# Layer 0's causal attention with the mLSTM head norms, the last modulation folds and half of tile 0's output projection placed inside it

## The chip, the cores and the metric

The kernel runs on one core of a Trainium2 chip. The metric is the device time of one execution in microseconds (us), lower is better. The engines are PE (TensorE, matrix products), DVE (VectorE), ACT (ScalarE), POOL (GpSimd) and SP (which only issues DMA transfers); each works through its own program in order, and they wait for each other by semaphores. Everything is float32.

## What is computed

Two blocks, 256 tokens of width 1024. Block 1 has two layers; the change lies in the mixer of layer 0, an mLSTM (4 heads of 128) beside a causal attention (8 heads of 64):

```python
h = rms_norm(x, norm_mix_g) * (1 + sc1) + sh1      # sh1, sc1, g1, sh2, sc2, g2 from silu(c) @ ada_w + ada_b
z = h @ w_in                                       # mq, mk, mv, mo, gates, bq, bk, bv
hm = mlstm_chunkwise(mq, mk, mv, i_pre, f_pre)
hm = rms_norm(hm, mnorm_g) * sigmoid(mo)           # per mLSTM head
qb, kb = rms_norm(bq, qn_g), rms_norm(bk, kn_g)    # per attention head
hb = softmax(qb @ kb.T / 8 - slope * distance, causal) @ bv     # 8 heads
x = x + g1 * (concat(hm, hb) @ w_out)
h = rms_norm(x, norm_ffn_g) * (1 + sc2) + sh2
x = x + g2 * peer_ffn(h)                           # 128 expert rows of u and v gathered per token
```

With 256 tokens and blocks of 256 keys, the reference's `moba_attention` has no past block to choose, so it is this plain causal attention. After it come layer 1 (differential attention, PEER again) and block 2 (three attentions and a mixture of experts).

## The kernel before

Tokens lie in two tiles of 128 (`T` = 2). `hT` holds the transposed input of the projections, 8 chunks of 128 features by 256 tokens; for the output projection `out0` chunks 0 to 3 are the mLSTM's heads and 4 to 7 the attention's, two heads in each. Every engine's program is written out by hand, so the order of the lines is the order of the work. What stands around the change, by line of the profile:

- **Projections.** `project` on PE (L946 to L988) and `move` on ACT (L1814) work through weight slots of 2 MB that SP loads into a ring of four (L741), each when its old user is done. `out0` is two slots of 512 columns, and per slot and tile 8 products 128x512 (L969). Two PSUM banks `gp` take turns.
- **Modulation of later layers.** Some vectors of `ada_w` are summed on DVE (`weigh`, L2516 to L2520, one per slot) and some on PE: the `mix` slots, 8 steps numbered 0 to 7, "part" (8 products, L946) or "fold" (2 products, L952 and L953). Steps 6 and 7 are folds.
- **mLSTM** (`mlstm`, PE L1248, ACT L1968, DVE L2572). For each of 4 heads: scores (L1258 to L1261), log weights on DVE (L2582), exp on ACT (L1976), weights (L2593), weights times values (L1280), and `divide` on DVE (L2601 to L2606), which writes the head into `y`. `mix` steps stand between the heads.
- **Norms of the attention's q and k.** Four blocks of 4 heads each (q 0 to 3, q 4 to 7, k 0 to 3, k 4 to 7). PE spreads the inverse roots over the rows (`head_spread`, L1060, through the two banks `tp`), DVE multiplies (`head_scale`, L2383).
- **Attention** (`attention("moba")`, PE L1170, ACT L1904, DVE L2465). One unit per head; per unit and tile: score products (L1182, four banks: two of `sp_`, two of `gp`), bias and row maximum on DVE (L2482, L2492), exp with row sum on ACT (L1928), reciprocal on DVE (L2499), division on POOL (`divide_rows`, L850), three transposes on PE (L1195, banks `tp`), copy by ACT (L1918, L1919), two value products per unit (L1209), and a copy of every pair of heads into `hT` by DVE (L2504). The loop keeps the transposes three units behind the scores. It begins when all q and k blocks are scaled and all `mix` steps moved.
- **mLSTM head norms.** Squares and sums on DVE ahead of the attention (L2627, L2628), the root on ACT (L1984), then `mlstm_scale` on DVE near the attention's end: per tile three passes of 128x512 (L2640 to L2642: times the inverse root, times `mnorm`, times the sigmoid `mo_sig`). PE turns the result into `hT` (L1014).
- **Behind it.** `out0` for tile 0 and tile 1, two `weigh` steps on DVE meanwhile, `first_residual` (L2648), `first_norm` (to L2662), the transposes of `h`, the queries of the PEER layer (`wq0`, L974), the top 16 of the scores (`topk`, L2668 to L2717), and the gather of expert rows by POOL (L909), 512 gathers of 1 MB over both layers.

## Time and profile before

| | before |
|---|---|
| median of 3 runs | 2408.13 us (2406.37 to 2408.23) |
| the profiled execution, its time | 2415.83 us |
| its span in the trace | 2414.0 us |
| PE busy | 2037.4 us, 84% |
| DVE busy | 1296.4 us, 54% |
| ACT busy | 835.6 us, 35% |
| POOL busy | 650.2 us, 27% |
| chain that ended last | PE 48%, DMA 35%, DVE 8%, ACT 6% |
| DMA | 932.78 MB, mean 386 GB/s |

The profile's page gives such totals over the whole span. The chain is followed back from the last instruction, each step to what released it. Since the stages have different limits, the timeline and the windows of the stage around the change (185 to 290 us) are what the next sections read. In a timeline row, "x8" counts records: a float32 product leaves two.

### The profile page before, as it was taken

To read this page: it belongs to the slowest core of one execution; us is meant where nothing else is said; L and a number is where in the kernel's file an instruction comes from. 1 tells how busy PE (TensorE), PEld (TensorE's weight loads), DVE (VectorE), ACT (ScalarE), POOL (GpSimd) and SP (SyncE) were. 2 spreads that over 40 slices of the span, in tenths; PEclk is the share of its full clock that TensorE was granted. 3 is DMA by queue.
4 is the path that set the end of the run, shared out by engine and by line. 5 is a ranking of instruction groups with operands and counts; after the bars stand their busy time and mean duration, and the time that the engine had idled before them with its cause. 6 is when DMAs were issued, how large, how long until landed. Compare 5 with 4: busy or idle time off the path is not lost.

```text
span 2414.0 us, 26478 instructions
## 1 busy us (share of the span) xinstructions
PE 2037.4 (84%) x9050; PEld 1072.1 (44%) x9050; DVE 1296.4 (54%) x3180; ACT 835.6 (35%) x2261; POOL 650.2 (27%) x601
## 2 busy tenths in 40 slices
PE   6997988798799899789989878988889996667676
PEld 3553732354265357256455423544447543222222
DVE  4866686767756775864867768455433421111111
ACT  1223254444534644443644435333323410000000
POOL 1001145433423433532433444434430300000000
PEclk9998999999999999999999999999999988888878
DMA  9984699999999999999999999999997269999998
GB/s 378 365 346 168 268 420 421 421 421 420 411 393 421 418 395 420 421 409 421 408 389 411 421 421 421 421 421 421 421 373 268 101 275 428 428 428 428 428 429 377
DMA packets 110268, 932.78 MB, mean 386 GB/s; under 512 B 12710, under 2 KB 14020, under 8 KB 16644
## 3 DMA queue, kind: packets, MB, share of 16 engines
q0 software_dynamic: 76800, 549.70, 55.6%
q1 hardware_dynamic: 33348, 381.60, 38.3%
q8 instruction: 61, 1.00, 0.2%
q14 instruction: 59, 0.48, 0.1%
HBM read 930.15 MB, written 6.06 MB: 388 GB/s over the span
## 4 chain that ended last, share of the span: by engine, by line
PE 48%; DMA 35%; DVE 8%; ACT 6%; issue 2%; POOL 1%; SPq 0%; DVEq 0%; POOLq 0%
DMA arena<-in_peer_uv_dram,arena 19%; PE summed L1323 18%; DMA arena<-in_moe_pieces_dram 15%; PE gp L1395 6%; PE gp L969 4%; DVE y_g L2733 4%; PE gp L988 2%; PE gp L1391 2%; PE gp L1686 2%; PE gp L979 2%; ACT arena L2019 1%; PE gp L1524 1%; PE gp L946 1%; ACT arena L2016 1%; PE gp L1073 1%
## 5 line engine op out<-in xcount | busy, mean ns | idle before, releaser
L1323 PE MATMUL summed<-arena 128*128 128x512 f32 x2048 | 987.4, 620 | 187.2 <-ACT arena L2019 165.8
L2733 DVE CUSTOM_DVE_ANT_0 y_g<-arena,h 128x1024 f32<-128x1024 f32 x512 | 627.1, 1225 | 409.2 <-DMA arena<-in_peer_uv_dram,arena 352.1
L909 POOL DMA_INDIRECT arena<-in_peer_uv_dram,arena x512 | 590.8, 1154 | 946.6 <-PE summed L1323 856.1
L1323 PEld LDWEIGHTS summed<-arena 128*128 128x128 f32 x2048 | 373.1, 195 | 699.5 <-ACT arena L2019 340.3
L2013 ACT ACTIVATE arena<-arena 128x1 f32<-128x1 f32 x512 | 102.2, 200 | 510.7 <-DVE arena L2733 509.8
L1686 PE MATMUL gp<-arena,mod 128*32 128x512 f32 x1008 | 161.6, 776 | 107.7 <-DMA arena<-in_moe_pieces_dram 107.7
L2019 ACT ACTIVATE arena<-cst,arena 128x128 f32<-128x128 f32 x512 | 205.5, 401 | 16.8
L3113 DVE TENSOR_TENSOR mod<-mod,gp 128x512 f32<-128x512 f32 x8 | 5.5, 688 | 367.5 <-ACT mod L2282 367.5
L2016 ACT ACTIVATE arena<-arena 128x1 f32<-128x1 f32 x512 | 150.8, 295 | 17.7 <-DVE arena L2722 1.1
L1686 PEld LDWEIGHTS gp<-arena,mod 128*32 128x32 f32 x1008 | 31.8, 126 | 229.3 <-DMA arena<-in_moe_pieces_dram 172.2
L969 PE MATMUL gp<-arena,hT 128*128 128x512 f32 x224 | 100.0, 606 | 1.1 <-issue 0.6
L2282 ACT ACTIVATE mod<-gp 128x512 f32<-128x512 f32 x8 | 4.8, 597 | 261.1 <-PE gp L1686 261.1
L1395 PEld LDWEIGHTS gp<-hT,mod 128*128 128x128 f32 x640 | 74.5, 192 | 9.8 <-issue 8.4
L1395 PEld LDWEIGHTS gp<-hT,arena 128*128 128x128 f32 x640 | 74.6, 192 | 9.6 <-issue 9.6
L2520 DVE SCALAR_TENSOR_TENSOR h<-arena,cst,h 128x512 f32<-128x512 f32 x98 | 73.7, 752 | 3.5
L1395 PE MATMUL gp<-hT,mod 128*128 128x128 f32 x640 | 74.8, 275 | 0.0
L1395 PE MATMUL gp<-hT,arena 128*128 128x128 f32 x640 | 74.7, 275 | 0.0
L969 PEld LDWEIGHTS gp<-arena,hT 128*128 128x128 f32 x224 | 43.0, 194 | 56.2 <-issue 55.2
L1814 ACT ACTIVATE arena<-gp 128x512 f32<-128x512 f32 (+1 forms) x29 | 17.1, 590 | 144.5 <-PE gp L988 41.2
L1661 PE MATMUL summed<-mod,h 128*128 128x128 f32 x256 | 46.3, 364 | 22.5 <-DVE mod L3108 22.4
L2668 DVE MAX8 arena<-arena 128x8 f32<-128x128 f32 (+1 forms) x192 | 58.4, 332 | 11.7 <-ACT arena L1998 8.4
L2013 ACT ACT_TABLE_LOAD x50 | 64.2, 1283 | 0.9
(468 smaller groups left out, 2162.3 us busy)
## 6 DMA issues: line engine op xcount, KB each, us to landing
arena<-in_moe_pieces_dram SPq DMA_DIRECT2D x95, 2048.0 KB, 25.6
arena<-in_w_slots_dram SPq DMA_DIRECT2D x47, 2048.0 KB, 10.1
arena<-in_w_parts_dram SPq DMA_DIRECT2D x45, 1024.0 KB, 9.2
mod<-in_w_parts_dram SPq DMA_DIRECT2D x29, 1024.0 KB, 9.3
arena<-in_peer_uv_dram,arena POOLq DMA_INDIRECT x512, 14.2
t_rep<-t_rows POOLq DMA_DIRECT2D x1, 3066.0 KB, 12.9
arena<-t_rep POOLq DMA_DIRECT2D x1, 2304.0 KB, 11.1
y_g<-in_moe_pieces_dram SPq DMA_DIRECT2D x1, 2048.0 KB, 17.8
```

What stands on the lines that cost most here:

```text
L909: pool.indirect_dma_start(rowbuf[b], None, a["peer_uv"].rearrange("l n d -> (l n) d"), bass.IndirectOffsetOnAxis(ap=idx[:, col(n):col(n) + ...
L969: mm = pe.matmul(bank, hT[:, k, grp[1] * P:(grp[1] + 1) * P], w[:, k, :], start=k == 0, stop=k == KT - 1)
L979: mm = pe.matmul(bank[:, c * P:(c + 1) * P], w[:, k, grp[1] + c * P:grp[1] + (c + 1) * P], hT[:, k, P:S], start=k == 0, stop=k == KT - 1)
L1323: mm = pe.matmul(op[:, b, :], diag[:, n % DIAGS, :], rowbuf[n % ROWS][:, D + b * 512:D + (b + 1) * 512], start=n % SLOTS == 0, stop=n % SL ...
L1395: mm = pe.matmul(bank[:, c * P:(c + 1) * P], w[:, k, c * P:(c + 1) * P], hT[:, k, tok], start=k == 0, stop=k == KT - 1)
L1686: mm = pe.matmul(gp[c, j, :], xe[:, 2 * kk + k, c], w[:, e, k, :], start=kk + k == 0, stop=kk == 3 and k == 1, skip_group_check=True)
L2013: link(act.activation(gelu[:, c:c + 1], dots[:, c:c + 1], ACT.Gelu))
L2016: link(act.activation(coef[:, c:c + 1], gelu[:, c:c + 1], ACT.Copy, scale=gate[:, c:c + 1]))
L2019: act.activation(diag[:, n % DIAGS, :], ident, ACT.Copy, scale=coef[:, c:c + 1]).then_inc(diag_ready, 1)
L2520: ins = v.scalar_tensor_tensor(out=acc, in0=w[:, k, :], scalar=cact[:, k:k + 1], in1=acc, op0=ALU.mult, op1=ALU.add)
L2668: ins = v.max(b[:, part], s)
L2733: v.tensor_tensor_reduce(y[:, t, :], rowbuf[n % ROWS][:, 0:D], h[:, t, :], 1.0, 0.0, ALU.mult, ALU.add, dots[:, c:c + 1]).then_inc(udot, 1)
```

## The change

All of it is order and placement in layer 0; the result is the same sum.

- **PE.** `mix` steps 6 and 7 leave the mLSTM, and the spreads of q 0 to 3 and k 0 to 3 stand there instead. `attention` becomes `causal_attention`, written out for pairs of heads: scores in the two `sp_` banks only, which leaves the `gp` banks to folds 6 and 7 and to two groups of `out0`. The first half (chunks 0 to 3, the mLSTM's part) of tile 0's two `out0` groups stands inside the attention, ahead of and behind the transposes of pair 2; the second halves follow the attention.
- **DVE.** The first two head scales stand before `divide(3)`, the others after the bias of pair 0. Squares are gone; the sums (`memory_squares`) and the scaling (`memory_scale`) stand inside the attention. Scaling is one pass per head of 128x128, because the `mnorm` factor is already in `mo_sig`.
- **POOL.** `gate_and_square` ahead of the divisions: `mo_sig` times `mnorm` (128x1024) and the two squares (128x512 each).
- **ACT.** The sigmoid comes before folds 6 and 7, the root of the head norms after the exps of pair 0, so there are two loads of the exp table in the attention. The order of the blocks in `QK` lets pairs 0 and 1 start after two blocks.

```diff
+causal = att["moba"][1]
+causal_home = [work[:, CH * j:CH * (j + 1)] for j in range(4)] + [tk[:, CH * j:CH * (j + 1)] for j in range(3)] + [work[:, 0:CH]]
...
-QK = {"moba": [(8, G_EVQ), (10, G_EVQ), (12, G_EVK), (14, G_EVK)],
+QK = {"moba": [(8, G_EVQ), (12, G_EVK), (10, G_EVQ), (14, G_EVK)],
...
+    def gate_and_square():
+        pool.wait_ge(sig_done, 1)
+        pool.wait_ge(lam_in, 48)
+        pool.tensor_tensor(mo_sig, mo_sig, mnorm.unsqueeze(1).to_broadcast([P, T, CH]), ALU.mult).then_inc(sig_done, 1)
+        pool.wait_ge(mm_read, M_HEADS)
+        for t in range(T):
+            pool.tensor_tensor(h[:, t, 0:CH], y[:, t, 0:CH], y[:, t, 0:CH], ALU.mult).then_inc(hn_sq, 1)
+    def divide_causal():
+        for j in range(len(causal)):
+            pool.wait_ge(d_inv, j + 1)
+                rows = causal_logits(j, t)
+                k = 2 * (j % 4) + t
+                ins = pool.tensor_tensor(rows, rows, den[:, k:k + 1].to_broadcast([P, (t + 1) * P]), ALU.mult)
...
+    def causal_scores(p):
+        pe.wait_ge(qk_done, 2 if p < 2 else 4)
+        for j in (2 * p, 2 * p + 1):
+            sg = causal[j]
+            if j >= 2:
+                pe.wait_ge(s_read, j - 1)
...
+    def causal_turn(p):
+        for j in (2 * p, 2 * p + 1):
+            pe.wait_ge(scale_ready, j + 1)
+            if j >= 2:
+                pe.wait_ge(t_moved, j - 1)
+            else:
+                pe.wait_ge(qk_done, 4)
...
+    def causal_values(p):
+        for j in (2 * p, 2 * p + 1):
+            pe.wait_ge(t_moved, j + 1)
+            if p >= 2:
+                pe.wait_ge(o_read, p - 1)
...
+    def turn_memory_out(t):
+        pe.wait_ge(ml_normed, t + 1)
+        pe.wait_ge(t_moved, 3 + 3 * t)
+        turn_rows(y[:, t, :], 1)
+    def out0_tile0(m, k0, k1):
+        n = phase_slots["out0"][m]
+        g = group_of[n, 0]
+        w = ring[:, place[n], :].rearrange("p (k c) -> p k c", k=KT)
+        if k0 == 0:
+            pe.wait_ge(w_landed[place[n]], 16 * (use[n] + 1))
+            pe.wait_ge(gemm_moved, g - 1)
+        for k in range(k0, k1):
+            mm = pe.matmul(gp[:, g % 2, :], hT[:, k, 0:P], w[:, k, :], start=k == 0, stop=k == KT - 1)
+        if k1 == KT:
+            mm.then_inc(gemm_done, 1)
+    def causal_attention():
+        causal_scores(0)
+        mix(6)
+        head_spread("moba", 2)
+        head_spread("moba", 3)
+        causal_scores(1)
+        mix(7)
+        causal_turn(0)
+        causal_scores(2)
+        causal_values(0)
+        causal_turn(1)
+        turn_memory_out(0)
+        causal_scores(3)
+        causal_values(1)
+        hT_ready()
+        out0_tile0(0, 0, 4)
+        causal_turn(2)
+        out0_tile0(1, 0, 4)
+        causal_values(2)
+        turn_memory_out(1)
+        hT_ready()
+        causal_turn(3)
+        causal_values(3)
...
-            mix(2 * hh + 1)
+                mix(2 * hh + 1)
+            else:
+                pe.wait_ge(mm_arg, M_HEADS)
+                head_spread("moba", 0)
+                head_spread("moba", 1)
...
-            mix(2 * hh + 2)
+            if hh < 2:
+                mix(2 * hh + 2)
...
-    pe.wait_ge(mm_arg, M_HEADS)
-    for i in range(len(QK["moba"])):
-        head_spread("moba", i)
-    pe.wait_ge(qk_done, len(QK["moba"]))
-    pe.wait_ge(gemm_moved, group_end(mix_slots[-1]))
-    attention("moba")
+    causal_attention()
-    for t in range(T):
-        project("out0", tile=t)
+    out0_tile0(0, 4, 8)
+    out0_tile0(1, 4, 8)
+    project("out0", tile=1)
...
+    def causal_attention():
+        causal_exp(0, 1)
+        mix(6)
+        act.wait_ge(hn_sq, 3)
+        act.activation(small[:, 32:40], small[:, 24:32], ACT.Sqrt).then_inc(hn_rt, 1)
+        mix(7)
+        causal_moved(0)
+        causal_exp(2, 3)
+        causal_moved(1)
+        causal_exp(4, 5)
+        move_turned_rows(0, 1)
+        causal_moved(2)
+        causal_exp(6, 7)
+        move_turned_rows(1, 1)
+        causal_moved(3)
...
-        mix(6)
-        mix(7)
-        act.wait_ge(hn_sq, 1)
-        act.activation(small[:, 32:40], small[:, 24:32], ACT.Sqrt).then_inc(hn_rt, 1)
...
+    def causal_bias(p):
+        for j in (2 * p, 2 * p + 1):
+            bias = causal[j]["bias"]
+            k = 2 * (j % 4)
+            v.wait_ge(s_done, j + 1)
+            if j == 7:
+                v.wait_ge(t_done, 1)
+            for t in range(T):
+                ins = v.scalar_tensor_tensor(out=causal_logits(j, t), in0=bias[1][t], scalar=bias[2],
+                                             in1=sp_[:, j % 2, t * S:t * S + (t + 1) * P], op0=ALU.mult, op1=ALU.add)
+            ins.then_inc(s_read, 1)
+            v.wait_ge(s_read, j + 1)
+            if j >= 4:
+                v.wait_ge(scale_ready, j - 3)
+            for t in range(T):
+                ins = v.tensor_reduce(nmax[:, k + t:k + t + 1], causal_logits(j, t), AX.X, ALU.max, negate=True)
+            ins.then_inc(m_done, 1)
...
+    def causal_attention():
+        causal_bias(0)
+        head_scale("moba", 2)
+        head_scale("moba", 3)
+        causal_inverse(0, 1)
+        memory_squares()
+        causal_bias(1)
+        memory_scale(0)
+        causal_inverse(2, 3)
+        causal_bias(2)
+        causal_out(0)
+        memory_scale(1)
+        causal_inverse(4, 5)
+        causal_out(1)
+        causal_bias(3)
+        causal_inverse(6, 7)
+        causal_out(2)
+        causal_out(3)
+        v.wait_ge(o_read, 4)
...
+        head_scale("moba", 0)
+        head_scale("moba", 1)
-        head_scales("moba")
-        yh = y[:, :, 0:512].rearrange("p t (h n) -> p t h n", h=M_HEADS)
+    def memory_squares():
-            link(v.tensor_tensor(sq[:, t], yh[:, t], yh[:, t], ALU.mult))
-            link(v.tensor_reduce(small[:, 24 + t * M_HEADS:24 + (t + 1) * M_HEADS], sq[:, t], AX.X, ALU.add))
+            v.wait_ge(hn_sq, t + 1)
+            ins = v.tensor_reduce(small[:, 24 + t * M_HEADS:24 + (t + 1) * M_HEADS], sq[:, t], AX.X, ALU.add)
+        link(ins)
-    def mlstm_scale():
-        yh = y[:, :, 0:512].rearrange("p t (h n) -> p t h n", h=M_HEADS)
-        v.wait_ge(hn_rt, 1)
-        link(v.reciprocal(small[:, 32:40], small[:, 32:40]))
-        r = small[:, 32:40].rearrange("p (t h) -> p t h", t=T)
-        v.wait_ge(sig_done, 1)
-        v.wait_ge(lam_in, 48)
-        for t in range(T):
-            link(v.tensor_tensor(yh[:, t], yh[:, t], r[:, t, :].unsqueeze(2).to_broadcast([P, M_HEADS, M_DH]), ALU.mult))
-            link(v.tensor_tensor(y[:, t, 0:512], y[:, t, 0:512], mnorm, ALU.mult))
-            link(v.tensor_tensor(y[:, t, 0:512], y[:, t, 0:512], mo_sig[:, t, :], ALU.mult))
-        v.sem_inc(ml_normed, 1)
+    def memory_scale(t):
+        if t == 0:
+            v.wait_ge(hn_rt, 1)
+            link(v.reciprocal(small[:, 32:40], small[:, 32:40]))
+            v.wait_ge(sig_done, 2)
+        for hh in range(M_HEADS):
+            rows = y[:, t, P * hh:P * (hh + 1)]
+            k = 32 + M_HEADS * t + hh
+            ins = v.scalar_tensor_tensor(out=rows, in0=rows, scalar=small[:, k:k + 1], in1=mo_sig[:, t, P * hh:P * (hh + 1)],
+                                         op0=ALU.mult, op1=ALU.mult)
+        ins.then_inc(ml_normed, 1)
```

On PE, from the values of mLSTM head 2 to the first scores; `summed` are the values, `gp` the folds, `turned` the spreads, `scores` the attention. Before:

```order
L1280 MATMUL summed<-ones,arena 128x1 x3
L952 MATMUL gp<-h,cst 1x512
L953 MATMUL gp<-ada_b,cst 1x512
L952 MATMUL gp<-h,cst 1x512
L953 MATMUL gp<-ada_b,cst 1x512
L1280 MATMUL summed<-arena 128x128 x3
L1280 MATMUL summed<-ones,arena 128x1 x3
L1060 MATMUL turned<-arena,cst 64x512 x8
L1182 MATMUL scores<-arena 128x128
```

Now:

```order
L1302 MATMUL summed<-ones,arena 128x1 x3
L1049 MATMUL turned<-arena,cst 64x512 x4
L1302 MATMUL summed<-arena 128x128 x3
L1302 MATMUL summed<-ones,arena 128x1 x3
L1167 MATMUL scores<-arena 128x128
L1167 MATMUL scores<-arena 128x256
L1167 MATMUL scores<-arena 128x128
L1167 MATMUL scores<-arena 128x256
L941 MATMUL gp<-h,cst 1x512
L942 MATMUL gp<-ada_b,cst 1x512
L1049 MATMUL turned<-arena,cst 64x512 x4
```

The two folds left the mLSTM, two of the four spreads took their place, and the first pair's scores stand ahead of a fold and of the other spreads.

On PE, the attention's last part; `turned<-cst,arena` are the weights of a pair, `summed` its values, `gp<-arena,hT` the output projection, `turned<-cst,y_g` the mLSTM's heads. Before:

```order
L1195 MATMUL turned<-cst,arena 128x128 x3
L1209 MATMUL summed<-y_g,arena 64x256
L1209 MATMUL summed<-y_g,arena 64x128
L1209 MATMUL summed<-y_g,arena 64x256
L1209 MATMUL summed<-y_g,arena 64x128
L1014 MATMUL turned<-cst,y_g 128x128 x8
L1209 MATMUL summed<-y_g,arena 64x256
L1209 MATMUL summed<-y_g,arena 64x128
L969 MATMUL gp<-arena,hT 128x512 x32
```

Now:

```order
L1213 MATMUL gp<-arena,hT 128x512 x4
L1181 MATMUL turned<-cst,arena 128x128 x6
L1213 MATMUL gp<-arena,hT 128x512 x4
L1194 MATMUL summed<-y_g,arena 64x256
L1194 MATMUL summed<-y_g,arena 64x128
L1194 MATMUL summed<-y_g,arena 64x256
L1194 MATMUL summed<-y_g,arena 64x128
L1003 MATMUL turned<-cst,y_g 128x128 x4
L1181 MATMUL turned<-cst,arena 128x128 x6
...
L1213 MATMUL gp<-arena,hT 128x512 x8
L958 MATMUL gp<-arena,hT 128x512 x16
```

Eight of the 32 products of `out0` now stand before the attention's end, around the transposes of pair 2, and the mLSTM's second tile is turned ahead of pair 3.

On ACT, the start of the attention; L1833 are the moves of the folds, L1948 the root of the head norms, L1940 and L1941 the copies of the turned weights, L1930 the exps:

```order
L2007 ACTIVATE arena<-arena 128x1024
L1930 ACT_TABLE_LOAD
L1930 ACTIVATE arena,den<-arena,nmax 128x128
...
L1833 ACTIVATE ada_rows<-gp 1x512
L1948 ACT_TABLE_LOAD
L1948 ACTIVATE small<-small 128x8
L1833 ACTIVATE ada_rows<-gp 1x512
L1940 ACTIVATE y_g<-turned 128x256
...
L1930 ACT_TABLE_LOAD
```

Before, the root stood ahead of all exps, with one load of the exp table behind it; now it stands between the exps of pairs 0 and 1, and the exp table is loaded twice.

## Rows read from the trace of the kernel before

**Rows 1.** Windows of two stages: us, PE, PEld, DVE, ACT, POOL busy (x), PEclk, DMA, GB/s.

```profile
198.00:227.00 29.00, 17.61 (x96) 10.97 (x96) 18.91 (x56) 14.09 (x52) 8.21 (x16) 0.74 0.05 19
...
285.00:1500.00 1215.00, 1065.56 (x3796) 560.32 (x3795) 852.84 (x2149) 559.28 (x1588) 488.51 (x425) 0.98 1.01 414
```

**Rows 2.** Chain of waits that ended last, from 200 us: start us, us, what.

```profile
201.13 1.28 ACT L1928
...
213.96 0.90 DVE y_g L2640
...
227.29 30.15 PE gp L969 x64
...
262.72 9.04 PE gp L974 x64
...
284.89 1.03 POOL arena L909
```

**Rows 3.** Timeline of PE from mLSTM head 2's values to the attention: start us, us, instruction.

```profile
185.93 0.94 PE L1280 MATMUL summed<-arena 128*128 128x128 f32 x6
...
187.36 1.02 PE L952 MATMUL gp<-h,cst 128*1 128x512 f32 x2
...
192.57 1.94 PE L1060 MATMUL turned<-arena,cst 128*64 128x512 f32 x8
...
198.71 0.93 PE L1182 MATMUL gp<-arena 64*128 64x128 f32 x8
...
204.72 0.76 PE L1195 MATMUL turned<-cst,arena 128*128 128x128 f32 x3 [5.08 <-POOL arena L850]
...
211.25 0.88 PE L1209 MATMUL summed<-y_g,arena 128*64 128x256 f32 x8
...
212.90 0.52 PE L1195 MATMUL turned<-cst,arena 128*128 128x128 f32 x3 [0.78 <-ACT y_g L1919]
```

**Rows 4.** Windows of PE alone in three stretches: us, PE busy (x), PEclk, DMA, GB/s.

```profile
205.00:208.30 3.30, 3.30 (x17) 0.50 0.00 0
...
215.40:232.20 16.80, 13.08 (x40) 0.50 0.06 9
...
232.20:258.00 25.80, 25.80 (x61) 1.00 0.66 244
```

**Rows 5.** Timeline of DVE, mLSTM head 3 to the ffn norm of tile 0.

```profile
192.68 0.16 DVE L2601 TENSOR_SCALAR small<-summed 128x2 f32<-128x2 f32 x1 [3.69 <-PE summed L1280]
...
194.36 1.41 DVE L2383 SCALAR_TENSOR_TENSOR arena<-arena,cst,turned 128x512 f32<-128x512 f32 x2 [0.16 <-DVE y_g L2606]
...
200.78 0.61 DVE L2482 SCALAR_TENSOR_TENSOR arena<-cst,scores 128x128 f32<-128x128 f32 x2
...
201.42 0.61 DVE L2492 TENSOR_REDUCE nmax<-arena 128x1 f32<-128x128 f32 x2
...
244.37 1.23 DVE L2648 TENSOR_TENSOR y_g<-y_g,mod 128x1024 f32<-128x1024 f32 x1 [3.58 <-ACT y_g L1814]
...
251.72 1.23 DVE L2662 TENSOR_TENSOR h<-h,mod 128x1024 f32<-128x1024 f32 x1
```

**Rows 6.** Timeline of ACT in the attention and the output projection.

```profile
202.42 0.40 ACT L1928 ACTIVATE arena<-arena,nmax 128x128 f32<-128x128 f32 x1
...
203.32 0.39 ACT L1928 ACTIVATE arena<-arena,nmax 128x128 f32<-128x128 f32 x1
...
205.81 0.38 ACT L1918 ACTIVATE y_g<-turned 128x256 f32<-128x256 f32 x1
...
243.74 0.60 ACT L1814 ACTIVATE y_g<-gp 128x512 f32<-128x512 f32 x1 [6.27 <-PE gp L969]
```

**Rows 7.** Timeline of POOL in the attention.

```profile
203.69 0.97 POOL L850 TENSOR_TENSOR arena<-arena,den 128x128 f32<-128x128 f32 x2 [115.77 <-DVE den L2499]
...
213.90 1.42 POOL L850 TENSOR_TENSOR arena<-arena,den 128x128 f32<-128x128 f32 x2 [1.34 <-DVE den L2499]
```

**Rows 8.** Timeline of SP's queue: the load that the second `weigh` releases.

```profile
240.82 0.33 SPq L741 DMA_DIRECT2D arena<-in_w_slots_dram  x1
```

More of the change, by code:

```diff
@@ new lines, in causal_exp, with causal_moved @@
+            def causal_exp(*units):
+                for u in units:
+                    act.wait_ge(m_done, u + 1)
+                    for t in range(T):
+                        lp = causal_logits(u, t)
+                        k = 2 * (u % 4) + t
+                        ins = act.activation(lp, lp, ACT.Exp, bias=nmax[:, k:k + 1], accum_out=den[:, k:k + 1])
+                    ins.then_inc(e_done, 1)
+            def causal_moved(p):
+                for j in (2 * p, 2 * p + 1):
+                    act.wait_ge(t_done, j + 1)
+                    if j >= 2:
+                        act.wait_ge(o_done, j - 1)
+                    pt = turned_p[j % 2]
+                    act.activation(pt[:, 0:S], tp[:, j % 2, 0:S], ACT.Copy)
+                    act.activation(pt[:, S + P:2 * S], tp[:, j % 2, S + P:2 * S], ACT.Copy).then_inc(t_moved, 1)
@@ L2222, in _ @@
             mlstm()
-            attention("moba")
+            causal_attention()
             move("out0", tile=0)
@@ new lines, in causal_inverse, with causal_out @@
+            def causal_inverse(*units):
+                for u in units:
+                    d = den[:, 2 * (u % 4):2 * (u % 4) + 2]
+                    v.wait_ge(e_done, u + 1)
+                    v.reciprocal(d, d).then_inc(d_inv, 1)
+            def causal_out(p):
+                v.wait_ge(o_done, 2 * p + 2)
+                v.tensor_copy(hT[:, 4 + p, :], op[:, p % 2, 0:S]).then_inc(o_read, 1)
+            def causal_attention():
[17 more added lines that the diff above has]
+                v.wait_ge(o_read, 4)
@@ L2967, in _ @@
             mlstm()
[L2968 removed]
+            causal_attention()
             v.sem_inc(y_ready, 1)
```

156 lines of the change are left out of this document (16 added, 140 removed).

## The prediction

> **What bounds the kernel now.** I read the windows by stage first. From 285 to 1500 us the DMA engines are busy all the time and move 414 GB/s; between 198 and 227 us they move 19 GB/s, PE is busy 17.61 of 29 us, and its clock is 0.74 [rows 1]. So the attention of layer 0 is no matter of bandwidth: it is a chain of short steps on four engines. The chain of waits says what hangs on it [rows 2]: a table load on ACT, the passes that scale the mLSTM's output on DVE, then the output projection as one block of 30.15 us on PE (227.29 to 257.44), `wq0` at 262.72, and the first gather on POOL at 284.89. The gathers move a fixed number of bytes at the full rate, so a first gather that is issued X us earlier should end the program X us earlier. The question is when the output projection ends, and whether what hangs on it can follow.
>
> PE's timeline shows what stands ahead of the attention [rows 3]: head 2's values take 1.43 us (185.93 to 187.36), and to the spreads at 192.57 it is 5.21 us more, which is head 3's values and two folds at 1.89 each. The clock windows show what the gaps do: PE waits 5.08 us for POOL before 204.72 [rows 3], waits again for some 2 us before 215.4, and both times its clock falls from 2.4 to 1.2 GHz, the second time until 232.2 us, well into the projection [rows 4]. One group of eight products takes 6.87 us at the full clock (6.27 idle and 0.60 busy of the ACT move that follows each group [rows 6]), so 32 would take 27.5 us; the 30.15 us contain 2.7 us of low clock.
>
> **The change, walked through.** Times are on the trace's clock; everything up to 187.36 us, the end of head 2's values, keeps its order.
>
> Step 1, the end of the mLSTM. Two spreads cost 1.94 us [rows 3] where two folds cost 3.78. Head 3's values end at 190.75 instead of 192.6. `divide(3)` takes 1.68 us (192.68 to 194.36 [rows 5]) and ends at 192.5.
>
> Step 2, PE's dense stretch: scores of pair 0 (0.93), fold (1.89), two spreads (1.94), scores of pair 1 (0.93), fold (1.89) [rows 3] from 190.75 to 198.35; six transposes (0.52 for three) to 199.4. The folds' 3.8 us are paid here, beside DVE: bias and maxima of a pair, 2.4 us (0.6 each for the bias and the maxima of a unit [rows 5]), from 192.5 to 194.85; two scales, 1.5; two reciprocals, 0.2; so 196.6. POOL starts 0.25 us later and takes 0.97 per unit [rows 7]: 198.8. Transposes find both weights ready. The squares that POOL now does are 512 elements each where 384 took 0.97 us, so 1.3 each or 2.6 in all, from 192.5 to 195.1, and `mo_sig` times `mnorm` another 2.6 before that; both are covered by the exps and scales up to 196.6. If POOL is as slow as in its one crowded row (1.42 against 0.97 [rows 7]) they end at 196.3, still in time. Beyond that, each us of POOL would be a us of pair 0.
>
> Step 3, ACT between pairs 0 and 1. Copies (0.38 for 256 columns [rows 6], 0.65 with the narrower one) to 200.3; a second load of the exp table, 1.28 us as in the chain [rows 2], to 201.6; exps of two units at 0.90 each [rows 6] to 203.4; reciprocal and POOL to 204.8; transposes to 205.4, copies to 206.0, exps of pair 2 to 207.8, copy of the mLSTM's first tile (0.60) to 208.4. The mLSTM's scaling (on the chain before, and in six passes of a tile's whole width) is now eight passes of a quarter of it between the biases; DVE has room, since pair 1 waits for ACT. PE idles about 3.5 us in all between 201.3 and 205.4. ACT's row follows on its table load without a gap.
>
> The Trainium skill ("ScalarE: Activation LUTs", section "What ACT_TABLE_LOAD costs") gives 1.28 us for the load and about 1.38 us more for a drain. This case's trace agrees with the first (1.28), and shows no drain: the load begins at 201.13 and the exp at 202.42. By the page the step would cost 1.4 us more, which the sum does without.
>
> Step 4, PE's second dense stretch: four products of `out0` (3.43), six transposes (1.04), four products (3.43), values of pair 2 (0.88), four transposes of the mLSTM's tile 1 (0.65), from 208.5 to 217.9; the copy and its hand-over 0.7; six transposes, the last copy and values, 2.3; the copy into `hT` and PE's restart 0.5: 221.4 us, where PE now begins the rest of `out0` (227.29 before). Exps, reciprocals and divisions of pair 3 take some 5 us beside the `out0` halves.
>
> Step 5, the rest of `out0` is 24 products instead of 32: 20.6 us, to 242.0 at the full clock. Before it was 257.44, so the sum is **15.4 us** if the clock never falls.
>
> Step 6, the clock. I expect it to fall once, in the gaps between 201.3 and 205.4, since in the trace it fell after the gap of 5.08 us and after the shorter one with little work around it [rows 3, 4]. Between about 205 and 211 us PE would then need twice its time; for the 5.5 us of work there that is +2.7 us, the same as the low clock costs the projection before. That leaves 12.7. Hand-overs that the walk rounds off, 0.1 to 0.3 us at some five places, take 0.7: **12.0 us** saved.
>
> Step 7, what follows the projection. DVE does two `weigh` steps after the attention. They run from 227.2 to 240.79 (3.58 idle before 244.37 [rows 5]), 13.6 us, and the norm to 252.95 takes 8.6. From 221.4 to 224 on, h would be ready at 243.6 to 246.2, while PE wants it 1.6 us after the projection's end, at 243.6 to 247. So DVE comes level and gives nothing away unless the clock stays full. SP issues a slot when the second `weigh` is done (240.82 [rows 8]) and the first slot of `wq0` after its `out0` slot; both move up by 6 and 12 us, and 4 MB at 414 GB/s are 10 us: landed by 248, needed at 251 (262.72 minus 12). The first gather moves from 284.89 to about 273. Downstream nothing is added.
>
> The sum is against the profiled execution: 2415.83 minus 12.0 is 2403.8. That one execution stands 7.7 us above the median of the runs, so the forecast of the median is 2408.13 minus 12.0, **2396.1 us**. A change under 0.2% (4.8 us) can't be told from none here.
>
> **The rivals.**
>
> The clock stays full (chance 0.12). PE's gap would be cut in two by pair 1's transposes, so it may not count as one. Then 15.4 us, and if the fall at `wq0` (9.04 us where the next one takes less) also goes, 17: 2391 to 2393. DVE's `weigh` steps bound it there.
>
> The clock stays low through the dense stretch (0.20). In the trace it was low for 16.8 us, of which PE was busy 13.08 [rows 4], and rose only in the projection. The first halves of `out0` now stand right behind a gap. If it stays low from 205 us to the end of tile 0, PE's work of 208.5 to 228 costs double except for its waits: the walk gives 252 us for the end of `out0`, 5 us saved, 2403; with an earlier rise 2399. The Trainium skill ("TensorE: Matmul & The Clock Gate", section "What's actually happening") has it that the low clock is the default and activity lifts it, which speaks against putting wide products behind gaps; the windows show the same fall and a slow rise.
>
> The gain is lost behind the projection (0.05). If DVE's `weigh` and norm, or `wq0`'s weights, or the scores' top 16 had no slack, the first gather would move by less than 4.8 us: 2404 to 2408. Against it: DVE waits 3.58 us now [rows 5], and moves up by the same 6 us as the attention's end, so it would have to lose 6 of its 9.5 us.
>
> Slower (0.03). Two score banks instead of four, and PE programs that wait in order, could put the pairs end to end. A pair's round is 0.5 (scores), 2.4, 1.8, 0.2, 2.2, 1.0, 0.7, 0.9, so 9.7 us; four of them from 190.8 are 229.6, the folds and spreads 5.7 and half projections 6.9 in the waits' way 242.2, and 20.6 us more end at 262.8, 5.4 us later: 2413.5. It decides once the scores of a pair wait for the values of the one before. The order shows them two steps ahead of those values, with only the bias of the pair between, so I give it little.
>
> The change not doing what it says is out: the order shows 8 products before the attention's end and 24 behind.
>
> **How the numbers follow.** My forecast, one fall of the clock, has 0.60. Its own bounds are 9 to 14 us saved: POOL at its crowded price and a late rise below, no rounding loss above. The range leaves out the low clock's worst end and the cases beyond it: 2391 to 2403 us. Faster by over 0.2% (under 2403.3): 0.60 and 0.12, and 0.17 of the low clock's 0.20, so 0.89. Within 0.2%: 0.03 and 0.05, so 0.08. Slower: 0.03.
>
> **What would show it.** Right: head 3's values end near 190.8; two loads of the exp table among the attention's exps; PE's `out0` in three pieces, the last of 24 products that begins near 222 and ends at 242 to 246; the first gather near 273 with windows of 414 GB/s behind it. POOL's squares should end before the first reciprocal. Wrong: transposes of pair 0 that wait for POOL beyond 200 us, a clock of 0.50 in the window behind 211 us, DVE still in its norm when PE waits for h, or a first gather that moves less than the projection's end.

## The result and the profile after

| | before | changed |
|---|---|---|
| median | 2408.23 us (2406.37 to 2411.36, 5 runs) | 2398.01 us (2391.68 to 2399.28, 5 runs) |
| ratio of the times | | 0.9939, 95% interval 0.9926 to 0.9951 |
| the profiled execution, time and span | 2415.83 and 2414.0 us | 2392.44 and 2390.5 us |
| PE, DVE, ACT, POOL busy | 2037.4, 1296.4, 835.6, 650.2 us | 2019.6, 1292.4, 836.0, 658.2 us |

The kernel is faster by 10.2 us in the medians. The ratio of the record isn't the quotient of the medians (0.9958), and its interval, 11.8 to 17.8 us, leaves that value out, so the size of the gain is known only to some 10 to 18 us. The forecast was 12.0 us and 2396.1, the range 2391 to 2403: right in its direction, and in the range.

The two profiled executions differ by 23.4 us, more than the change is worth. Head 2's values start at 182.0 us in the changed kernel and at 185.9 before, though nothing ahead of them changed but the order of two blocks. So from here on intervals are counted from the start of head 2's values ("head 2", 185.93 in [rows 3]), which takes the start of the execution out.

PE in the changed kernel, its timeline from head 2 to the queries (the last bracket is the idle time before, and what ended it):

```profile
185.29 0.94 PE L1302 MATMUL summed<-arena 128*128 128x128 f32 x6
...
186.72 0.93 PE L1167 MATMUL scores<-arena 64*128 64x128 f32 x8
...
194.10 0.98 PE L1181 MATMUL turned<-cst,arena 128*128 128x128 f32 x6
...
199.51 0.55 PE L1181 MATMUL turned<-cst,arena 128*128 128x128 f32 x3 [2.09 <-POOL arena L838]
...
204.39 3.91 PE L1213 MATMUL gp<-arena,hT 128*128 128x512 f32 x8
208.13 0.82 PE L1181 MATMUL turned<-cst,arena 128*128 128x128 f32 x6
208.79 3.60 PE L1213 MATMUL gp<-arena,hT 128*128 128x512 f32 x8
...
217.58 7.10 PE L1213 MATMUL gp<-arena,hT 128*128 128x512 f32 x16 [0.61 <-DVE hT L2511]
224.52 13.90 PE L958 MATMUL gp<-arena,hT 128*128 128x512 f32 x32
...
243.70 7.41 PE L963 MATMUL gp<-hT,arena 128*128 128x128 f32 x64 [1.35 <-ACT arena L2012]
...
253.03 1.10 PE L953 MATMUL gp<-y_g,ones 128*128 128x512 f32 x2 [1.06 <-DVE y_g L2547]
```

Head 3's values come 3.3 us after head 2's (5.2 before [rows 3]), the first scores right behind them, and pair 0's transposes wait for nobody. The one long gap is 2.09 us before pair 1. The rest of `out0` starts 35.6 us after head 2 (41.4 before) and takes 20.8 us for 24 products; 32 took 30.15 [rows 2]. The clock, in windows of PE alone (us, busy, granted clock, DMA share, GB/s):

```profile
196.00:201.30 5.30, 2.83 (x22) 1.00 0.02 6
201.30:204.60 3.30, 3.30 (x19) 0.52 0.00 0
204.60:241.50 36.90, 34.94 (x108) 1.00 0.44 164
```

In this stretch it fell once, behind that gap, to 1.2 GHz for some 3.3 us, and was back at about 204.8 us, 0.4 us into the first wide products (204.39, 3.91 us for 3.60 in the next group). Before, it was low for 3.3 and again for 16.8 us [rows 4]. The `wq0` block at 243.70 ran at the full clock; before, it took 9.04 us at 262.72 [rows 2].

ACT and POOL in the timeline of the changed kernel:

```profile
192.77 1.28 ACT L1948 ACT_TABLE_LOAD   x1
...
195.93 1.28 ACT L1930 ACT_TABLE_LOAD   x1
197.22 0.40 ACT L1930 ACTIVATE arena<-arena,nmax 128x128 f32<-128x128 f32 x1
```

```profile
185.18 2.35 POOL L826 TENSOR_TENSOR arena<-arena 128x1024 f32<-128x1024 f32 x1 [100.13 <-ACT arena L2007]
188.66 2.04 POOL L829 TENSOR_TENSOR h<-y_g 128x512 f32<-128x512 f32 x2 [1.13 <-DVEq L2635]
192.59 1.90 POOL L838 TENSOR_TENSOR arena<-arena,den 128x128 f32<-128x128 f32 x4 [1.88 <-DVE den L2506]
```

The second exp table costs 1.28 us and the exp follows at once (195.93 and 197.22), so the drain of about 1.38 us that the Trainium skill gives ("ScalarE: Activation LUTs", section "What ACT_TABLE_LOAD costs") is not seen here either. POOL's squares took 2.04 us (2.6 forecast) and ended 1.88 us before the first division.

DVE behind the attention:

```profile
210.55 0.17 DVE L2506 RECIPROCAL den<-den 128x2 f32<-128x2 f32 x1 [3.24 <-ACT arena L1930]
...
217.01 0.42 DVE L2511 COPY hT<-summed 128x256 f32<-128x256 f32 x1 [3.30 <-PE summed L1194]
217.58 0.49 DVE L2543 TENSOR_SCALAR h<-arena,cst 128x512 f32<-128x512 f32 x1
...
230.95 1.22 DVE L2678 TENSOR_TENSOR y_g<-y_g,mod 128x1024 f32<-128x1024 f32 x1
...
238.29 1.23 DVE L2692 TENSOR_TENSOR h<-h,mod 128x1024 f32<-128x1024 f32 x1
...
255.76 0.49 DVE L2698 MAX8 arena<-arena 128x8 f32<-128x128 f32 x2 [2.35 <-ACT arena L2021]
```

The residual waits for nothing now (3.58 us before [rows 5]): DVE works from 217.6 to 253.4 us with one pause of 0.22 us, and the chain of waits runs through it, not through PE's projection:

```profile
217.58 0.50 DVE h L2543
...
265.45 1.03 POOL arena L898
```

The first gather starts 83.4 us after head 2; before it was 99.0 (284.89 [rows 2] less 185.93 [rows 3]). That is 15.5 us: 5.8 in the attention, 9.3 in the projection (8 products fewer, 6.9 us, and the low clock), 0.4 behind.

### The profile page after: what moved, and what is told of

Its sections match the earlier page's. It is cut to its first block, busy times and chain, and to the rows that moved or that the text cites. A ratio compares the mean times of both kernels' runs of the same rounds, so it can differ in the third digit from the quotient of the medians.

```text
span 2390.5 us, 26484 instructions
## 1 busy us (share of the span) xinstructions
PE 2019.6 (84%) x9050; PEld 1064.1 (45%) x9050; DVE 1292.4 (54%) x3180; ACT 836.0 (35%) x2262; POOL 658.2 (28%) x604
## 4 chain that ended last, share of the span: by engine, by line
PE 47%; DMA 36%; DVE 9%; ACT 5%; issue 2%; POOL 1%; SPq 0%; DVEq 0%; POOLq 0%
DMA arena<-in_peer_uv_dram,arena 20%; PE summed L1346 18%; DMA arena<-in_moe_pieces_dram 15%; PE gp L1418 6%; DVE y_g L2763 4%; PE gp L958 3%; PE gp L977 2%; PE gp L1414 2%; PE gp L1705 2%; PE gp L968 2%; PE gp L1547 1%; ACT arena L2042 1%; PE gp L935 1%; ACT arena L2039 1%; PE turned L1049 1%
## 5 line engine op out<-in xcount | busy, mean ns | idle before, releaser
L958 PE MATMUL gp<-arena,hT 128*128 128x512 f32 x192 | 83.7, 594 | 0.5 <-DVE hT L2431 0.5
L1833 ACT ACTIVATE arena<-gp 128x512 f32<-128x512 f32 (+1 forms) x29 | 17.1, 590 | 141.3 <-PE gp L977 41.2
L2701 DVE FIND_INDEX8 arena<-arena 128x8 uint32<-128x128 f32 (+1 forms) x192 | 61.7, 330 | 0.0
```

Of the source, the lines that this page charges most:

```text
L958: mm = pe.matmul(bank, hT[:, k, grp[1] * P:(grp[1] + 1) * P], w[:, k, :], start=k == 0, stop=k == KT - 1)
L2701: ins = v.max_index(w[:, part], b[:, part], s)
```

## The experiments

Each kernel is the changed one with the edit named. The times of kernels with different starts scatter by 6 to 10 us, so each has two readings: the interval from head 2 to the first gather in its profile, and the median beside that of the kernel before on the same chip.

| kernel | attention's end | projection's end | first gather | median us, before | ratio (95%) |
|---|---|---|---|---|---|
| before (first profile) | 41.3 | 71.4 | 99.0 | | |
| before again | 41.4 | 71.5 | 99.1 | 2410.65, 2411.67 | 1.0002 (0.9992 to 1.0012) |
| changed | 35.4 | 56.4 | 83.4 | 2398.01, 2408.23 | 0.9939 (0.9926 to 0.9951) |
| changed again | 35.4 | 56.3 | 83.8 | 2399.70, 2410.37 | 0.9949 (0.9936 to 0.9963) |
| tile 0's products behind | 29.9 | 57.6 | 83.5 | 2400.30, 2410.37 | 0.9952 (0.9936 to 0.9968) |
| folds back | 41.1 | 62.0 | 89.1 | 2401.52, 2410.37 | 0.9961 (0.9947 to 0.9975) |
| squares on DVE | 37.9 | 58.9 | 85.9 | 2394.57, 2410.37 | 0.9933 (0.9918 to 0.9948) |
| three passes | 35.5 | 56.4 | 83.5 | 2398.06, 2411.66 | 0.9938 (0.9920 to 0.9957) |
| all four back | 36.3 | 64.1 | 91.6 | 2402.53, 2411.67 | 0.9959 (0.9944 to 0.9974) |
| 8 products more | 35.0 | 62.8 | 90.3 | 2407.23, 2411.66 | 0.9977 (0.9965 to 0.9988) |
| gap filled | 34.7 | 55.6 | 82.7 | 2395.57, 2411.66 | 0.9934 (0.9918 to 0.9949) |
| weigh inside | 35.0 | 56.0 | 83.5 | 2397.02, 2411.67 | 0.9937 (0.9922 to 0.9953) |
| best | 35.4 | 56.4 | 80.5 | 2393.06, 2411.66 | 0.9919 (0.9903 to 0.9935) |
| best, gap filled | 34.7 | 55.6 | 79.8 | 2393.51, 2411.67 | 0.9924 (0.9910 to 0.9939) |

(Columns 2 to 4: us from the start of head 2's values to DVE's last copy into `hT`, to the first product behind `out0`, and to the first gather. One profile stands behind each row. In the rows where `wq0`'s first block ran partly at the low clock, 9.04 us for 7.41, the first gather holds 1.6 us of it: both rows of before, changed again, all four back, 8 products more, weigh inside.)

**Both kernels again**, unchanged.

> The changed kernel once more, unchanged, with a second profile. Theory A (the walk: a gain in the attention reaches the end one for one, and single executions scatter by some 6 us for reasons elsewhere, such as the start of the kernel): the median lies 8 to 16 us below the kernel before, and the time from the values of mLSTM head 2 to the end of the attention in the new profile is again about 35.5 us (41.4 before), from there to the first gather about 47.9. Theory B (the gain is partly given back behind the attention because DVE's four weigh steps bound what follows): the same median, but the interval from the attention's end to the first gather is longer than before by several us.

> The kernel before, unchanged, for a second profile of it. If the 15.5 us between the two first profiles (start of head 2's values to first gather, 99.0 against 83.4) are the change's and not one execution's, this interval is again 97 to 100 us, and the ratio of the times is 1.000 within 0.2%.

The intervals repeat within 0.4 us (83.4 and 83.8; 99.0 and 99.1) while the starts do not (182.0 and 186.8; 185.9 and 182.3). So the 15.2 to 15.5 us are the change's, and the start belongs to the execution. Theory A holds; B's longer interval behind the attention is not there (48.0 and 48.4, against 57.7 before).

The second profile is not the same in all: `wq0`'s first block took 9.04 us, and PE waited for no `weigh` step behind it.

```profile
248.49 9.04 PE L963 MATMUL gp<-hT,arena 128*128 128x128 f32 x64 [1.35 <-ACT arena L2012]
257.37 1.97 PE L953 MATMUL gp<-y_g,ones 128*128 128x512 f32 x4
```

Behind the same gap of 1.35 us the clock fell in this profile and not in the first. So a fall there belongs to the execution. It makes PE late enough that the fourth `weigh` step is done in time: the wait of 1.06 us shows in the first profile only.

**Tile 0's products behind the attention.**

```diff
                 hT_ready()
-                out0_tile0(0, 0, 4)
                 causal_turn(2)
-                out0_tile0(1, 0, 4)
...
-            out0_tile0(0, 4, 8)
-            out0_tile0(1, 4, 8)
+            out0_tile0(0, 0, 8)
+            out0_tile0(1, 0, 8)
```

> The changed kernel, but with all 8 products of both out0 groups of tile 0 behind the attention. A: the attention ends 5 to 6 us earlier because pairs 2 and 3 no longer stand behind 6.9 us of projection, and the projection ends 1.5 us later, or 4.5 us later if the wider gaps bring the low clock; the time is 1 to 4 us above the changed kernel. A reading that counts 8 products as a gain of 6.9 us expects 6.9 us more. B: 0 or less, since DVE's weigh steps begin 5 us earlier and they bound.

The attention ends 5.5 us earlier and the projection 1.3 us later, as A had it, but the first gather does not move (83.5), and the median is 0.6 us above the changed kernel's second set, not 1 to 4. The reading of 6.9 us falls. PE in this kernel, and its clock around the same gap:

```profile
205.06 0.55 PE L1181 MATMUL turned<-cst,arena 128*128 128x128 f32 x3 [2.09 <-POOL arena L838]
...
217.50 13.97 PE L1213 MATMUL gp<-arena,hT 128*128 128x512 f32 x32 [0.56 <-issue]
231.31 13.90 PE L958 MATMUL gp<-arena,hT 128*128 128x512 f32 x32
...
250.49 7.41 PE L963 MATMUL gp<-hT,arena 128*128 128x128 f32 x64 [1.35 <-ACT arena L2010]
257.74 1.98 PE L953 MATMUL gp<-y_g,ones 128*128 128x512 f32 x4
```

```profile
203.00:206.00 3.00, 0.55 (x4) 1.00 0.00 0
206.00:217.50 11.50, 8.40 (x55) 1.00 0.00 0
```

All 32 products ran at the full clock, 27.6 us, and the last row waits for no `weigh` step. But this profile has no low clock between 200 and 258 us, neither behind the gap of 2.09 us nor in `wq0`, so the changed kernel's row is no fair match. The kernel with the gap filled (below) is the changed one without a fall: against it the projection ends 2.0 us later here (57.6 and 55.6) and the first gather 0.8 us later (83.5 and 82.7). There PE waited 1.00 us for the fourth `weigh` step, here it didn't: the earlier end of the attention lets DVE make up more than half of what PE loses. The part of the change that its name puts forward last is worth some 0.8 us at the gather, on one profile each.

**Folds 6 and 7 back in the mLSTM** (PE and ACT both).

```diff
+                        mix(7)
                         pe.wait_ge(mm_arg, M_HEADS)
...
-                    if hh < 2:
+                    if hh < 3:
                         mix(2 * hh + 2)
...
                 causal_scores(0)
-                mix(6)
...
                 causal_scores(1)
-                mix(7)
...
                 causal_exp(0, 1)
-                mix(6)
...
+                mix(6)
+                mix(7)
                 act.activation(mo_sig, zn[:, :, 512:1024], ACT.Sigmoid).then_inc(sig_done, 1)
```

> The changed kernel, but folds 6 and 7 stand again between the mLSTM's heads on PE and ACT. A: head 3's values come 3.8 us later, the attention ends 3.5 us later, and the time is 3 to 4 us above the changed kernel. B: under 1.5 us, since DVE behind the attention has slack or bounds.

Head 3's values come 3.8 us later, as A had it, but the attention ends 5.7 us later, not 3.5, and the first gather 5.6 us. Most of the difference has its place in `divide(3)` on DVE. ACT now moves both folds ahead of the sigmoid, so POOL's multiplication of the gate runs beside `divide(3)`, and one small product of it takes 1.73 us and ends with POOL's:

```profile
190.50 2.35 POOL L826 TENSOR_TENSOR arena<-arena 128x1024 f32<-128x1024 f32 x1 [105.66 <-ACT arena L2006]
```

```profile
191.13 1.73 DVE L2629 TENSOR_TENSOR small<-small 128x2 f32<-128x2 f32 x1
```

In the changed kernel the same product took 0.34 us, also ending with POOL's (187.56 and 187.53), and 0.16 in the kernel with three passes, where POOL does not multiply the gate. So the first bias comes 5.2 us later than in the changed kernel (11.9 us after head 2 for 6.7), before any low clock. The clock falls too, amid PE's waits for DVE and POOL at 193 to 199 us:

```profile
182.00:196.30 14.30, 12.80 (x67) 1.00 0.94 401
196.30:210.00 13.70, 10.93 (x47) 0.50 0.01 4
210.00:230.00 20.00, 18.39 (x70) 1.00 0.05 8
```

These are 13.7 us at 1.2 GHz against 3.3, but from the first bias to the attention's end this kernel takes only 0.5 us more than the changed one (29.2 and 28.7 us), so the low clock cost at most about that much: PE waits for other engines there. The median is 1.8 us above the changed kernel's second set, inside its scatter.

**Squares on DVE, and three passes of scaling.** In the first, POOL only multiplies the gate; in the second it does only the squares.

```diff
-                pool.wait_ge(mm_read, M_HEADS)
-                for t in range(T):
-                    pool.tensor_tensor(h[:, t, 0:CH], y[:, t, 0:CH], y[:, t, 0:CH], ALU.mult).then_inc(hn_sq, 1)
...
-                    v.wait_ge(hn_sq, t + 1)
+                    link(v.tensor_tensor(h[:, t, 0:CH], y[:, t, 0:CH], y[:, t, 0:CH], ALU.mult))
```

```diff
-                pool.tensor_tensor(mo_sig, mo_sig, mnorm.unsqueeze(1).to_broadcast([P, T, CH]), ALU.mult).then_inc(sig_done, 1)
...
-                for hh in range(M_HEADS):
-                    rows = y[:, t, P * hh:P * (hh + 1)]
-                    k = 32 + M_HEADS * t + hh
-                    ins = v.scalar_tensor_tensor(out=rows, in0=rows, scalar=small[:, k:k + 1], in1=mo_sig[:, t, P * hh:P * (hh + 1)],
-                                                 op0=ALU.mult, op1=ALU.mult)
-                ins.then_inc(ml_normed, 1)
...
+                link(v.tensor_tensor(yh[:, t], yh[:, t], r[:, t, :].unsqueeze(2).to_broadcast([P, M_HEADS, M_DH]), ALU.mult))
+                link(v.tensor_tensor(y[:, t, 0:512], y[:, t, 0:512], mnorm, ALU.mult))
+                v.tensor_tensor(y[:, t, 0:512], y[:, t, 0:512], mo_sig[:, t, :], ALU.mult).then_inc(ml_normed, 1)
```

> The changed kernel, but the squares of the mLSTM head norms are on DVE again (two more passes of 0.7 us before the bias of pair 1), POOL only multiplies the gate. A: the root comes 1.4 us later and, because ACT works in order, the copies of pair 0 and the exps of pair 1 too: 1 to 1.5 us above the changed kernel. Rival: DVE waited at that place anyway (0.67 us before the reciprocal of pair 1), so 0 to 0.5 us, or less than 0 if POOL's squares slowed DVE.

> The changed kernel, but POOL does not multiply the gate by mnorm, and memory_scale runs three passes of 128x512 per tile on DVE as before (2.1 us for 1.13). A: for tile 0 DVE has about 0.7 us of room before the reciprocal of pair 1, for tile 1 none before the reciprocal of pair 2, so the attention ends 0 to 1.5 us later; the fused scaling is not where the gain is. Rival: the six passes on the chain were a main part of the time before (4.8 us), so 2 us or more.

The squares cost 2.5 us in the interval, more than A's 1.5. Up to POOL's division of pair 1 the loss is 1.4 us, as A had it: the root comes later, and ACT's copies of pair 0's weights and the exps with it. The other 1.1 us come between there and the attention's end, where PE's clock stays low for longer:

```profile
190.00:201.90 11.90, 10.78 (x56) 1.00 0.84 358
201.90:212.00 10.10, 9.33 (x39) 0.50 0.00 0
212.00:245.00 33.00, 31.39 (x96) 1.00 0.39 139
```

That the clock is their whole cause is not shown. Yet the median is the lowest of the single undoings, 5.1 us under the changed kernel's on the same chip, with intervals that overlap. Its profile makes up the time behind the gather (2121.4 us to the end, where the others take 2124 to 2130). One profile each can't tell whether that is the version or the execution; it stays open. The three passes cost nothing (35.5 and 83.5).

**All four back together.**

> The changed kernel with four parts undone together: folds in the mLSTM, squares on DVE, three passes of scaling, all products of tile 0 behind the attention. What is left of the change is the attention written in pairs, with its first scores and exps ahead of the second q and k blocks and of the head norms. A: the parts overlap (each covers a wait that the others leave), so the interval from head 2's values to the first gather lies between the single undoings and the kernel before, at 90 to 94 us (83.6 changed, 99.0 before), and the time 5 to 9 us above the changed kernel. Rival (the gain is the sum of the parts undone singly, 5.7, 2.5, 0 and 0): 91.8 from the sum with nothing for the overlap, and if the order in pairs is worth nothing, 99.

91.6 is in A's band, and is also what the rival's addition gave (91.8): the two readings aren't told apart by it. What is left of the change (the order in pairs, with the spreads of the first blocks and the exps moved ahead of the root) takes 7.4 us off (99.0 to 91.6): 5.0 in the attention, and 2.4 in the projection, whose 32 products ran at the full clock (27.7 us for 30.1). The remaining 7.8 us (to 83.8, the profile with the same low clock in `wq0`) come from the four parts. How they share it is open: the 5.7 of the folds holds 1.4 us of `divide(3)` waiting for POOL's multiplication, which this kernel doesn't have; its first bias comes 3.6 us later than in the changed kernel, not 5.2.

**8 products more**, between the attention and the projection.

```diff
+            for _ in range(8):
+                pe.matmul(sp_[:, 0, :], ident, cst[:, 0:512], start=True, stop=True)
             out0_tile0(0, 4, 8)
```

> The changed kernel with 8 extra products 128x512 (a result that nobody reads) on PE between the attention and the rest of the output projection. They cost 6.9 us on PE and nothing on DVE. A (what PE gains or loses before the projection's end reaches the first gather and the end of the program): the first gather comes 5 to 6 us later (6.9 less the 1.1 us that PE waited for the fourth weigh step), and the time is 5 to 6 us above the changed kernel. B (DVE's weigh steps bound): the first gather comes at most 3 us later.

The first gather came 6.5 to 6.9 us after the changed kernel's (90.3), the median 7.5 us above that of its second set (from another chip) and 9.2 above that of its first. A's carry holds: what PE loses there reaches the end. A's 1.06 us of slack did not show: in this profile `wq0`'s first block ran partly at the low clock (9.04 us for 7.41), as in the changed kernel's second profile, where PE waited for no `weigh` step either. B falls.

**The gap filled.**

```diff
                 causal_values(0)
+                pe.wait_ge(gemm_moved, group_of[phase_slots["out0"][0], 0] - 1)
+                for _ in range(2):
+                    pe.matmul(gp[:, group_of[phase_slots["out0"][0], 0] % 2, :], ident, cst[:, 0:512], start=True, stop=True)
                 causal_turn(1)
```

> The changed kernel with 2 extra products 128x512 (1.7 us, result overwritten) in PE's gap of 2.1 us before the transposes of pair 1. If the fall of the clock near 201 us comes from that gap, the windows from 200 to 212 us stay at 1.00 and the attention ends 1 to 1.5 us earlier than with the changed kernel (34 to 34.5 us after the start of head 2's values, against 35.5). If the fall has another cause, 35.5 or up to 1 us more.

```profile
196.00:201.00 5.00, 4.76 (x23) 1.00 0.23 95
201.00:206.00 5.00, 3.94 (x26) 1.00 0.00 0
206.00:241.00 35.00, 33.39 (x106) 1.00 0.45 166
```

The clock did not fall, and the attention ended 0.7 us earlier (1 to 1.5 expected). The windows in which PE was idle behind pair 0's values now hold the fillers, and the best version with fillers (below) had no fall there either. Without them the clock fell behind this gap (2.1 to 2.3 us) in six profiles and stayed up in one, that of tile 0's products behind, whose PE program is the same up to there. So the gap is needed for the fall as far as these show, but doesn't always bring it. The price of this fall is 0.7 us and not the 1.7 that 3.3 us at half the clock lose: at the full clock PE waits 0.75 us for ACT's copy of the mLSTM's first tile ahead of the wide products (204.71 us), which it didn't in the changed kernel.

**A better version**, first with one of its three moves alone.

```diff
                 causal_bias(3)
+                weigh_start(16, 4)
                 causal_inverse(6, 7)
+                weigh_rest(16, 4, KT)
                 causal_out(2)
...
-            for i in range(16, 18):
-                weigh(i)
+            weigh(17)
...
+                pe.wait_ge(gemm_moved, group_of[phase_slots["wq0"][m], 0] + 1)
+                score_first(m)
                 if m == 0:
                     project("vec", slice(14, 16))
-                pe.wait_ge(gemm_moved, group_of[phase_slots["wq0"][m], 0] + 1)
-                score_first(m)
...
+            move_keys(0)
             act.wait_ge(lam_s, 1)
             act.activation(small[:, 42:44], small[:, 40:42], ACT.Exp).then_inc(lam_e, 1)
-            move_keys(0)
```

(The first two pieces are the `weigh` step, on DVE, split into `weigh_start` and `weigh_rest`, whose bodies are left out here; the third is on PE, with ACT's moves in the same order; the fourth is on ACT.)

> The changed kernel with only the first of the three moves of the best version: one weigh step in DVE's idle time in the attention. A: DVE's bound behind the attention goes away (PE no longer waits 1.06 us for the fourth weigh step), but ACT's table load ahead of wq0 stays: first gather at 82 to 82.7 us after head 2's values (83.6 changed, 80.6 best). Rival: all of the best version's 3 us come from it.

> The changed kernel with three moves behind what the new trace shows as the bound from 217 us on, DVE: the first of the four late weigh steps is done in DVE's idle time inside the attention (half before and half after the reciprocals of pair 3); PE scores the first queries before it sums the last two vectors; ACT copies the keys before it loads the exp table for lambda. A: the attention's end stays (0 to 0.5 us later), the first gather comes 3 to 4 us earlier (79 to 81 us after the start of head 2's values, against 83.6), and the time is 3 to 4 us below the changed kernel. Rival: PE's projection bounds anyway, so 0 to 1.5 us.

> The best version with the 2 filler products in PE's gap. If the fillers keep the clock up as in fill_gap, the attention ends 0.7 us earlier (34.7 after head 2's values) and the first gather is at 79.8 to 80.2; the time is 0.5 to 1 us below best, which is less than the scatter. If not, as best.

The weigh step alone left the first gather at 83.5, where A expected 82 to 82.7; its first `wq0` block ran partly at the low clock (9.04 us for 7.41, 1.6 us), so it would be some 81.9 without that fall, an estimate and not a measurement. Like with like, it lies 0.3 us below the changed kernel's second profile, which had the same fall, and all of that is the attention's end. All three moves give 80.5, 2.9 us less than the changed kernel's first profile, both with `wq0` at the full clock; with the fillers 79.8. So the rival, that all of it comes from the `weigh` step, isn't borne out: by the estimate the step is about half of it. DVE in the best version has its `weigh` step around the reciprocals, and then waits:

```profile
210.49 2.33 DVE L2555 SCALAR_TENSOR_TENSOR h<-arena,cst,h 128x512 f32<-128x512 f32 x3
212.84 0.17 DVE L2506 RECIPROCAL den<-den 128x2 f32<-128x2 f32 x1
213.17 0.17 DVE L2506 RECIPROCAL den<-den 128x2 f32<-128x2 f32 x1 [0.16 <-ACT arena L1930]
213.25 3.63 DVE L2555 SCALAR_TENSOR_TENSOR h<-arena,cst,h 128x512 f32<-128x512 f32 x4
...
254.58 0.49 DVE L2719 MAX8 arena<-arena 128x8 f32<-128x128 f32 x2 [5.01 <-ACT arena L2021]
```

Its median is 2393.06 us with a ratio of 0.9919 (0.9903 to 0.9935): below the changed kernel's 0.9939 and 0.9949. The interval overlaps that of the first set (from 0.9926) and ends just below the second (from 0.9936), and the sets ran on different chips, so the gain over the changed kernel rests on the intervals in the traces. The fillers add nothing that the times can show (0.9924).

## Why the prediction held, step by step

- **Step 1** (end of the mLSTM): right. Head 3's values 3.3 us after head 2's, as walked.
- **Step 2** (dense stretch): right. POOL was over-priced (2.04 us for 2.6, and 2.35 for 2.6) and did not matter. The folds between the scores cost nothing there: undoing them brings head 3's values 3.8 us later, the whole of their time. The rest of that run's 5.7 us is `divide(3)` waiting for POOL (1.4) and only some 0.5 with the low clock.
- **Step 3** (ACT between pairs 0 and 1): right, 1.28 us for the table load and a gap in PE before pair 1; with 2.09 us and 0.38 between the two units it was shorter than the 3.5 in all that I gave.
- **Step 4** (second dense stretch): the start of the rest of `out0` was walked to 34.0 us after the end of head 2's values at the full clock; it is 34.1 (35.6 from their start), with a fall of the clock in it. But crediting the 8 moved products with their 6.9 us would have been wrong: at equal clock the run with them behind gathers 0.8 us later.
- **Step 5**: right, 20.8 us for 20.6.
- **Step 6** (clock): the term that was mis-sized. One fall was forecast and came, but for 3.3 us and not 6, and it cost 0.7 us (gap filled), not 2.7, because it met transposes and scores, half of it in time that PE would have waited for ACT, and was over 0.4 us into the wide products. The working is also at odds with itself: twice the time for 5.5 us of work is 5.5 us more; 2.7 is what a stretch of 5.5 us at half the clock loses. And the 0.7 us for hand-overs have no counterpart: the attention moved by 5.8 us where the walk had 5.9 without clock and hand-overs.
- **Step 7**: that DVE "comes level and gives nothing away" failed in the first profile. The step counted the two `weigh` steps ahead of the residual and not the two behind the norm. `h` was ready in time (239.5 us, PE's transposes at 240.05), but the fourth `weigh` step held PE for 1.06 us, and the chain of waits went over to DVE from 217.6 us on. The sum hid this: `wq0`'s first block regained 1.6 us of clock in that profile.
- **The sum**: 12.0 us were forecast, and the first gather moved by 15.5, to 269.4 us on the clock of the trace before, not 273. That this is so near the 15.4 of the full clock is errors that cancel (0.7 of low clock against 0.5 behind the projection and roundings). That the median, 2398.01, lies 1.9 us from the forecast is luck in part: with 0.7 us of low clock and no hand-overs the same sum gives 2393.4 us, 4.6 below it.
- **From the gather to the end**: the carry was tested (plus 6.6 us at the gather, plus 7.5 in the median). The medians of the change itself show 10.2 and 10.7 us where the gather moved by 15.5; the upper ends of the ratios' intervals, 17.8 and 15.4, reach it or nearly. With executions that scatter by 8 us and start 4 to 5 us apart, the traces show nothing given back in the gathers: from the first gather to the end it is 2129.1 and 2125.7 us before, 2125.1 and 2128.2 changed. Why the medians moved less stays open.
- **Rivals**: the full clock would have been 15.4 us, which is the size that the intervals show, though the clock did fall; the low clock through the dense stretch did not happen in the changed kernel, but did in the folds run (13.7 us) and the squares run (10.1 us). The slower rival was far off.

## What to carry to other kernels

When a chain of small steps on several engines is rewritten, put work of the same engine that nobody waits for (here two folds) into the gaps of the matrix engine: its time leaves the chain, here 3.8 us. Count a low clock only where that engine is the bound: 13.7 us of it cost some 0.5 us in one run. When an engine's work moves, look at what now runs beside it: POOL's multiplication held a small product of DVE for 1.73 us. Ask of a block that is moved earlier which engine is the bound behind it; half a projection inside the attention brought PE 2.0 us and the gather 0.8, since DVE held the rest. And where executions scatter more than the change, measure between two events of the same trace, one ahead of the change and one behind.

## What was not expected of the hardware

- The granted clock stayed at 1.2 GHz for 10 to 14 us while PE was busy 9.33 of 10.10 us (squares on DVE) or 10.93 of 13.70 (folds back), with scores, transposes and values of 64 columns; in the changed kernel the same sort of work had it back after 3.3 us.
- The same gap did not always bring the low clock: behind 1.35 us of idle time `wq0`'s first block took 9.04 us in six profiles (both of before among them) and 7.41 in five, and the changed kernel shows both.
- A DVE product of 128x2 took 0.16 us by itself, and 0.34 us (changed) and 1.73 us (folds back) beside a POOL product of 128x1024; both times the two ended within 0.03 us of each other.
- The start of an execution differs by 4 to 5 us between profiles of one kernel (head 2's values at 182.0 and 186.8, at 182.3 and 185.9).
